# Row sums on VectorE alone with two operand blocks kept in fp32, the bias rows in GpSimd's queue, prompt rows behind a quarter of the compression weights, and the window copies one batch at a time

## What is computed

```python
shift, scale, gate = jnp.split(c @ ada_w + ada_b, 3, axis=-1)
h = rmsnorm(x, norm_g) * (1 + scale[:, None, :]) + shift[:, None, :]
return split_proj(h @ w_in), gate          # q, three K/V pairs, gates, conv inputs, z
...
k_cmp, v_cmp = compress(kc, *cmpw[:3]), compress(vc, *cmpw[3:])
lg = jnp.einsum('bqghd,bngd->bghqn', qs, k_cmp) + tab[t5_bucket(d_cmp)].transpose(2, 3, 0, 1)
...
new_kw = jnp.concatenate([buf_kw, kw], axis=1)[:, -nbuf:]
new_vw = jnp.concatenate([buf_vw, vw], axis=1)[:, -nbuf:]
```

## Time and profile before

| | us |
|---|---|
| median of three runs | 1560.9 (1558.49 to 1562.39) |
| the profiled execution | 1560.68 |
| its span, first to last instruction | 1558.9 |
| PE busy | 1440.9 (92%) |
| DVE busy | 969.7 (62%) |
| ACT busy | 704.3 (45%) |
| POOL busy | 255.4 (16%) |
| mean granted TensorE clock | 0.969 of full |

### The profile page before, as it was taken

How to read it: one execution, slowest core, us unless ns; L and a number is a source line. 1 busy time by engine, 2 the same in 40 slices (tenths; PEclk the granted TensorE clock), 3 DMA queues, 4 the chain that set the end, 5 groups by cost and what they waited for, 6 DMA issues and landing times.

```text
span 1558.9 us, 27902 instructions
## 1 busy us (share of the span) xinstructions
PE 1440.9 (92%) x10526; PEld 1242.7 (80%) x10526; DVE 969.7 (62%) x2302; ACT 704.3 (45%) x1546; POOL 255.4 (16%) x446
## 2 busy tenths in 40 slices
PE   4499988999999999949989988999998999899998
PEld 2498988999999999948777767777777776688886
DVE  2344778787887887837676646666667655553226
ACT  2222223323323233217567767777777775641111
POOL 1101332101001011031013132131131132000000
PEclk9699998999999999969999999999999999999999
DMA  9843123333333333297321231011111019973231
GB/s 353 114 131 93 31 64 86 97 76 103 83 83 110 76 89 108 51 321 233 109 90 58 59 123 40 29 45 38 28 42 42 29 38 367 253 228 94 83 98 35
DMA packets 170677, 164.76 MB, mean 106 GB/s; under 512 B 53484, under 2 KB 151916, under 8 KB 165360
## 3 DMA queue, kind: packets, MB, share of 16 engines
q1 hardware_dynamic: 155968, 97.25, 23.9%
q0 software_dynamic: 14576, 65.73, 12.4%
HBM read 131.27 MB, written 35.83 MB: 107 GB/s over the span
## 4 chain that ended last, share of the span: by engine, by line
PE 76%; DMA 7%; DVE 7%; SPq 4%; ACT 3%; issue 3%; POOL 0%; DVEq 0%; ACTq 0%; POOLq 0%
PE PS L1269 27%; PE PS L1630 11%; PE PS L1436 7%; PE PS L1401 6%; PE PS L1380 4%; PE PS L1318 4%; PE PS L1381 3%; DMA gw<-in_ada_w 2%; PE PS L1225 1%; PE PS L1226 1%; PE PS L1227 1%; DMA kb<-in_cache_k_slc,idxs 1%; PE PS L1483 1%; SPq L794 1%; DMA mixed<-mixs 1%
## 5 line engine op out<-in xcount | busy, mean ns | idle before, releaser
L1269 PE MATMUL PS<-bo,wsl 128*128 128x264 f32 x4104 | 508.2, 287 | 13.7 <-DVE qp L2180 8.3
L1269 PEld LDWEIGHTS PS<-bo,wsl 128*128 128x128 f32 x4104 | 506.4, 191 | 15.8 <-DVE qp L2180 8.7
L1890 ACT ACTIVATE pr<-PS,nm 128x640 f32<-128x640 f32 (+7 forms) x256 | 181.4, 710 | 46.3 <-DVE nm L2383 44.0
L1913 ACT ACTIVATE ptt<-PS 128x512 f32<-128x512 f32 x264 | 149.9, 602 | 47.9 <-PE PS L1401 47.6
L1726 ACT ACTIVATE wsl<-wsum 128x512 fp32r<-128x512 f32 x105 | 65.6, 630 | 228.4 <-DVE wsum L2115 228.4
L1401 PE MATMUL PS<-ident,pr 128*128 128x128 f32 x1056 | 147.6, 274 | 0.0
L1436 PE MATMUL PS<-ptt,kvt 128*64 128x256 f32 x1056 | 138.6, 394 | 3.3 <-DVE mixs L2423 3.3
L1401 PEld LDWEIGHTS PS<-ident,pr 128*128 128x128 f32 x1056 | 122.8, 141 | 8.8 <-ACT ptt L1913 0.4
L1436 PEld LDWEIGHTS PS<-ptt,kvt 128*64 128x64 f32 x1056 | 67.6, 137 | 45.2 <-issue 20.9
L2383 DVE CUSTOM_DVE_ANT_0 PS<-PS,near,nm 128x256 f32<-128x256 f32 x192 | 94.7, 493 | 6.8
L2382 DVE TENSOR_REDUCE nm<-PS 128x1 f32<-128x128 f32 (+5 forms) x128 | 70.5, 551 | 40.3 <-PE PS L1381 39.5
(11 more groups left out here) (350 smaller groups left out, 2413.0 us busy)
## 6 DMA issues: line engine op xcount, KB each, us to landing
wr<-in_w_in SPq DMA_DIRECT2D x32, 512.0 KB, 5.4
adaw<-in_ada_w SPq DMA_DIRECT2D x8, 1024.0 KB, 9.4
wr<-in_w_in SPq DMA_DIRECT2D x32, 256.0 KB, 4.4
q_stacked<-qp POOLq DMA_DIRECT2D x64, 128.0 KB, 2.7
qb<-q_stacked SPq DMA_DIRECT2D x32, 256.0 KB, 3.1
mr<-mixed SPq DMA_DIRECT2D x16, 512.0 KB, 3.9
mixed<-yy POOLq DMA_DIRECT2D x16, 264.0 KB
xb<-in_x_prompt POOLq DMA_DIRECT2D x8, 512.0 KB, 5.1
```

Of the source, the lines that this page charges most:

```text
L1269: ins = pe.matmul(PS[:, 2 * q + c, 0:H // 2], w[:, x, kk, :], b[:, y, kk, c * H // 2:(c + 1) * H // 2], start=(first and kk == 0 and x == ...
L1890: act.activation(pr[r][:, h, 0:k], score_cols(b0, w), ACT.Exp, scale=-1.0, bias=nm[:, r, h:h + 1], accum_out=rsum[:, r, h:h + 1]).then_inc ...
L1913: act.activation(pt[tc % NPT5][:, :, :], PS[:, turn_bank(c), :].rearrange("p (h c) -> p h c", h=4), ACT.Copy).then_inc(pt_act, 1)
```

## The change

Five things are altered.

1. **Bias rows.** The DMA `bias_rows<-rows` leaves SP's queue and stands in POOL's, behind the load of the last `xb` tile and ahead of the stores of kc and vc. The wait for it leaves SP's `load_w(0)` and stands before `near` on SP and before ScalarE's first write into `ca` at product (0, 5).
2. **Row sums.** POOL's `low_sums` is gone. VectorE makes `whole(O22)`, the four pieces of O22's high plus low part in fp32, in `qp` (4 instructions ahead of the gate's additions), and `whole(O11)` over them before piece 12 (4 more). A piece x < 18 is then two additions: high part with the kept piece, and the low part. Pieces 18 and 19 take three. `PIECES` is altered, and the last eight pieces are made in another order (`PIECE`), so that those which use `qp`'s upper half come first; ScalarE's `query_high` of group 2 waits for `op_sum` 16 and 18, since it writes `qp`.
3. **Prompt rows.** SP issues one quarter of the weights, then the twelve DMAs of the rows, then the other three quarters.
4. **Gather.** Quarter 1 moves from behind (23, 4) to behind (23, 6) and all of group 23's stores.
5. **Window copies.** `store_window(which, b)` copies one buffer, behind units 4 to 19; the sample's rows go behind unit 20.

```diff
         tb_mm, tb_ev, tb_rel = sem("tb_mm"), sem("tb_ev"), sem("tb_rel")
-        low_sum, op_hi = ct_pe, tb_mm
+        op_kept, op_hi = tail_t, tb_mm
...
             return tuple(m for m in prepared_at(n, i) if is_sum(m))
-        PIECES = {(0, 0): 0, (0, 1): 1, (0, 3): 2, (0, 4): 3, (0, 5): 4, (0, 7): 5, (1, 0): 6, (1, 2): 7, (1, 3): 8, (1, 4): 9,
-                  (1, 5): 10, (1, 7): 11, (2, 2): 12, (2, 3): 13, (2, 4): 14, (2, 5): 15, (2, 6): 16, (2, 7): 17, (3, 0): 18, (3, 1): 19}
+        PIECE = [(s_, k) for s_ in range(3) for k in range(HK)] + [(3, 2), (3, 3), (4, 2), (4, 3), (3, 0), (3, 1), (4, 0), (4, 1)]
+        PIECES = {(0, 0): 0, (0, 1): 1, (0, 2): 2, (0, 3): 3, (0, 4): 4, (0, 5): 5, (0, 6): 6, (0, 7): 7, (1, 0): 8, (1, 4): 9,
+                  (1, 5): 10, (1, 6): 11, (2, 2): 12, (2, 3): 13, (2, 4): 14, (2, 5): 15, (2, 6): 16, (2, 7): 17, (3, 0): 18, (3, 1): 19}
...
             sp.wait_ge(wk_ld, 32)
-            sp.wait_ge(tb_ev, 1)
-            rv = rows[:, :]
-            sp.dma_start(rowd, bass.AP(rv.tensor, rv.offset, [list(rv.ap[0]), [0, P], [1, XW]])).then_inc(row_st, 16)
...
             sp.wait_ge(wk_lo, 2)
-            sp.wait_ge(row_st, 16)
...
             sp.wait_ge(*made(NBLK - 1, 2))
-            for q in range(4):
-                load_w1(0, q)
+            load_w1(0, 0)
             sp.wait_ge(xz, 1)
...
                 load_rows(0, r)
+            for q in range(1, 4):
+                load_w1(0, q)
...
             sp.wait_ge(x3_t, 80)
+            sp.wait_ge(row_st, 16)
...
                 po.dma_start(xb[s % 2][0:rows_of(tile_at(s)), :], xp[:, s - 1, :] if s else xs).then_inc(x_ld[s % 2], 16)
+            po.wait_ge(tb_ev, 1)
+            rv = rows[:, :]
+            po.dma_start(rowd, bass.AP(rv.tensor, rv.offset, [list(rv.ap[0]), [0, P], [1, XW]])).then_inc(row_st, 16)
...
                     nout[0] += 16
-            def store_window(which):
+            def store_window(which, b):
                 dst, buf, col = ((s_kw, cache_k_win, C_KW), (s_vw, cache_v_win, C_VW))[which]
-                po.dma_start(dst[0, :, 0:WIN - TS, :, :].rearrange("b t g d -> b (t g d)"),
-                             buf[0, :, TS:WIN, :, :].rearrange("b t g d -> b (t g d)")).then_inc(out_st, 16)
-                for b in range(NB):
-                    po.dma_start(dst[0, b, WIN - TS:WIN, :, :].rearrange("t g d -> t (g d)"),
-                                 kvs[TS * b:TS * b + TS, col:col + DKV]).then_inc(out_st, 16)
-                nout[0] += 16 * 9
+                po.dma_start(dst[0, b, 0:WIN - TS, :, :], buf[0, b, TS:WIN, :, :]).then_inc(out_st, 16)
+                po.dma_start(dst[0, b, WIN - TS:WIN, :, :].rearrange("t g d -> t (g d)"),
+                             kvs[TS * b:TS * b + TS, col:col + DKV]).then_inc(out_st, 16)
+                nout[0] += 32
             store_rows(0)
...
             def gather_quarter(c, q):
-                if c == 0 and q < 2:
-                    po.wait_ge(*made(NBLK - 1, 1 if q == 0 else 4))
+                if c == 0 and q == 0:
+                    po.wait_ge(*made(NBLK - 1, 1))
...
             po.wait_ge(h_lo, NTT)
-            def low_sums(x):
-                dst, a, b, op = SUMS[x // 4]
-                if x >= 2:
-                    po.wait_ge(op_sum, x - 1)
-                po.tensor_tensor(op_scratch(x)[1][:, :], f32(bo[a][:, 1, x % 4, :]), f32(bo[b][:, 1, x % 4, :]), op).then_inc(low_sum, 1)
...
                 for i in range(products(n)):
-                    if (n, i) in PIECES:
-                        x = PIECES[n, i]
-                        if x == 0:
-                            po.wait_ge(ada_mm, 2 * KC)
-                        low_sums(x)
...
                         gather_quarter(0, 0)
-                    if n == NBLK - 1 and i == 5:
-                        gather_quarter(0, 1)
             store_za(NBLK - 1, 0)
...
             po.wait_ge(*made(NBLK - 1, 6))
+            gather_quarter(0, 1)
...
                     first(u + 1)
-                if u in (2, 5):
-                    store_window(u // 3)
-                if u == 8:
+                if 4 <= u < 4 + 2 * NB:
+                    store_window((u - 4) // NB, u % NB)
+                if u == 4 + 2 * NB:
...
                         if n == NPLAIN and i >= 2:
-                            pe.wait_ge(op_lo, {2: 4, 3: 8, 4: 16, 5: 12, 6: 20}[i])
+                            pe.wait_ge(op_lo, {2: 4, 3: 8, 4: 18, 5: 12, 6: 20}[i])
...
                 elif x >= 12:
-                    act.wait_ge(*made(2, 1))
-                act.activation(bo[SUMS[x // 4][0]][:, 0, x % 4, :], op_scratch(x)[0][:, :], ACT.Copy).then_inc(op_hi, 1)
+                    act.wait_ge(*made(2, 3 if PIECE[x][0] == 4 else 1))
+                act.activation(bo[SUMS[PIECE[x][0]][0]][:, 0, PIECE[x][1], :], op_scratch(x)[0][:, :], ACT.Copy).then_inc(op_hi, 1)
...
                     act.wait_ge(q_st, 128 * (n // 3))
+                else:
+                    act.wait_ge(op_sum, 16 if half else 18)
...
                     act.wait_ge(g_st, 16)
+                    act.wait_ge(row_st, 16)
...
                 dve.tensor_tensor(wsl[m % NSLOT][:, 1, :, :], source(m), f32(wsl[m % NSLOT][:, 0, :, :]), ALU.subtract).then_inc(w_lo, 1)
+            def whole(block):
+                for k in range(HK):
+                    ins = dve.tensor_tensor(f32(qp[:, k, :]), f32(bo[block][:, 0, k, :]), f32(bo[block][:, 1, k, :]), ALU.add)
+                ins.then_inc(op_kept, 1)
             def op_add(x):
-                dst, a, b, op = SUMS[x // 4]
+                s_, k = PIECE[x]
+                dst, a, b, op = SUMS[s_]
                 t = op_scratch(x)
...
                     dve.wait_ge(op_lo, x - 1)
-                link(dve.tensor_tensor(t[0][:, :], f32(bo[a][:, 0, x % 4, :]), f32(bo[b][:, 0, x % 4, :]), op))
-                dve.wait_ge(low_sum, 1 + x + 1)
-                dve.tensor_tensor(t[0][:, :], t[0][:, :], t[1][:, :], ALU.add).then_inc(op_sum, 1)
+                if x < 18:
+                    dve.wait_ge(op_kept, 1 if x < 12 else 2)
+                    first_, second = (f32(bo[a][:, 0, k, :]), f32(qp[:, k, :])) if s_ < 4 else (f32(qp[:, k, :]), f32(bo[b][:, 0, k, :]))
+                    link(dve.tensor_tensor(t[0][:, :], first_, second, op))
+                    dve.tensor_tensor(t[0][:, :], t[0][:, :], f32(bo[a if s_ < 4 else b][:, 1, k, :]), ALU.add).then_inc(op_sum, 1)
+                else:
+                    dve.tensor_tensor(t[0][:, :], f32(bo[a][:, 0, k, :]), f32(bo[b][:, 0, k, :]), op)
+                    link(dve.tensor_tensor(t[1][:, :], f32(bo[a][:, 1, k, :]), f32(bo[b][:, 1, k, :]), op))
+                    dve.tensor_tensor(t[0][:, :], t[0][:, :], t[1][:, :], ALU.add).then_inc(op_sum, 1)
             def op_low(x):
-                dst, t = bo[SUMS[x // 4][0]], op_scratch(x)
+                (s_, k), t = PIECE[x], op_scratch(x)
+                dst = bo[SUMS[s_][0]]
                 dve.wait_ge(op_sum, x + 1)
                 dve.wait_ge(op_hi, 1 + x + 1)
-                dve.tensor_tensor(dst[:, 1, x % 4, :], t[0][:, :], f32(dst[:, 0, x % 4, :]), ALU.subtract).then_inc(op_lo, 1)
+                dve.tensor_tensor(dst[:, 1, k, :], t[0][:, :], f32(dst[:, 0, k, :]), ALU.subtract).then_inc(op_lo, 1)
...
             link(dve.memset(uu[:, 0, 0:2], 0.0))
+            whole(O22)
...
                             op_low(x - 1)
+                        if x == 12:
+                            whole(O11)
...
                 ev_late(NBLK - 1, i)
-            dve.wait_ge(tail_t, 1)
+            dve.wait_ge(tail_t, 2 + 1)
```

## The result

The changed kernel takes 1536.06 us (median of 4 runs, 1532.23 to 1538.53) where the kernel before, on the same chip, takes 1559.7. The ratio is 0.9846, with a 95% interval of 0.9818 to 0.9874. Faster was right; the time lies above the range of 1504 to 1529. Timed once more beside other kernels it gave 1536.74 us and 0.984 (0.9813 to 0.9868).

A forecast was written before the change was run, and what follows sets the result against it. PE, busy 1440.9 of 1558.9 us, was taken as the bound, with its waits to be cut. Terms -21.8 + 3.0 - 10.7 - 12 - 6 = -47.5 on 1560.7 gave 1513 us, range 1504 to 1529.

The forecast's parts named there:

- Part 1: Projection's gates: the first gate load's 20.0 us wait and 1.8 us of slow restart go, later gate loads cost 0; -21.8 us.
- The end of the range: Gates: bound where a gate load beside the bias rows lands 10 us late, plus a slow restart; 11 us lost.
- Part 2: First products: `whole(O22)` delays the start, +3.0 us; within the stage, stretched VectorE instructions and PE gaps shrink, -10.7 us.
- Parts 3 and 4: Compression's start: prompt rows land earlier, their wait shrinks to 2 us, first `pair` at 682 to 683 us; -12 us.
- My end of -5: Compression's start, worst bound: quarter 1's gather takes the DMA engines first, weights come at 690 us; only -5 us.
- no tighter: Compression: stores needed before ScalarE's fifth step land near 687 us, after POOL's memset near 682, leaving the margin unchanged.
- Part 5: Attention: spread window copies remove PE's waits of 3.3 us on `mixs` and 2.7 us on `wide`; -6 us.
- the +12: Attention, worst bound: POOL's 1.0 us of issues shows up each time in short units; 12 us lost.
- Rivals 1 and 2: Gate loads starve beside bias rows, 1524 us, chance 0.22; compression weights come last and late, 1520, chance 0.15; both 1531.
- Rival 3: Attention: POOL's two issues in each of 16 units delay `wide`; price up to 18 us, 1531 us, chance 0.06.
- rival 4: Product (1, 0): bias rows land late for ScalarE's `ca` and the kc and vc stores; slower, 1566 us, chance 0.02.
- rival 5: Products stage: VectorE stays stretched by POOL's stores; price 11 us, 1524 us, chance 0.06.

The follow-up runs named there:

- the kernel with 16 copies: Changed kernel with 16 copies of the bias rows in place of 128, and `near` loaded as eight loads of 16 partitions; 1517.26 us, ratio 0.9721.
- `whole` was moved: Changed kernel with the four additions of `whole` for the first block put behind the four gate additions on VectorE; 1531.93 us, ratio 0.9793.
- the run with the gather held back: Changed kernel with the second quarter's gather issued only when all four quarters of the compression's first weights have landed; 1536.26 us, ratio 0.9835.
- the quarter semaphores: Changed kernel with a semaphore for each quarter of the compression's weights, so the first pair waits for the first quarter alone; 1531.04 us, ratio 0.98.
- the late copy: Changed kernel with GpSimd issuing the bias rows' copy behind the gates' store, after the last gate load; 1538.91 us, ratio 0.9844.
- the copy in two steps: Changed kernel with the bias rows copied once from SBUF to DRAM, then 127 times from DRAM to DRAM; 1525.42 us, ratio 0.9759.

## Why the prediction was wrong, point by point

**Part 1, -21.8 forecast, -6.9 measured: here the prediction failed.** The wait of 20.0 us went as said. The step that failed is "I take 0" for the three gate loads beside the bias rows. One of them, k = 5, cost 12.3 us of wait and 1.4 us of slow restart: 22.90 us from 98.38 to 121.28 and 11.96 to 133.24, where both periods are 10.58 us in the kernel with 16 copies. After the wait the clock was granted at 0.50 from 121 to 124 us. That is 13.7 us of the 14.9 that are missing; of the 14.7 us that come back with 16 copies, 1.1 us had come before the wait (its gates of k = 4 are at 97.27). The end of the range was right in its mechanism and low in its size (11 in place of 13.7). What led me wrong was the row by which I chose: small loads among gathers of 8 KB pieces late in the program said that a newcomer in SyncE's queue is served in between, where the one row of *this* copy beside a load of *this* size said 20.1 us. I set it aside because the queues were the other way round. They don't matter: 20.1 us one way, 22.25 us the other.

**Part 2.** The start: +3.0 forecast, +1.96 measured as the growth of PE's wait (2.0 less again when `whole` was moved). Within: -10.7 forecast, -8.8 measured (95.90 us from the first product to the one behind the gap, now 87.08). All stretched instructions are back at 0.7 us and one gap is left, as forecast, but of 5.76 us and not 2.4. The release named there, `qp`, is as forecast. Its size was wrong by 3.4 us, the rest of the stage made good 1.5. The cause was right too, as the row sums alone show. But the row that the prediction called in agreement does not show it: at 211.52 us VectorE began ahead of POOL's addition (211.84), so that row does not say which held the other.

**Parts 3 and 4, -12 forecast, -4.7 measured (552.7 to 548.0 us from the gap's product to the attention).** The second step that failed. The rows came on time: the wait for them is 1.5 us, 2 were forecast. The weights were issued from 660 us, and the forecast had them through some 9 us behind the tails; they took 14.06 us, and the pair stood at 16.8 us behind the tails (660.09 to 676.85). My end of -5 is where it came out; it named the gather, and the run with the gather held back shows that 6 us of the 12.4 are indeed the gather's. But a first pair on time would not have given 12 either. With the quarter semaphores it stood 7.5 us behind the tails, better than forecast, and the stage gave 8.0 us in all (552.7 to 544.7): the stores ahead of the fifth step, which the prediction called "no tighter", landed 18.2 us behind the tails (681.36, tails at 663.13), where it had them 14 behind (687 and 673.32), and PE stood 4.2 us for them. The term missed what the loads and stores do to each other while the DMA engines are 95 to 99% busy. That this load is why the weights and stores are slow is argued from the table by stretch, not shown by a run of its own.

**Part 5, -6 forecast, -8.6 measured alone.** Both waits gone, no trace of the +12. The two waits are 6.0 us of it. For the rest there is the clock, which stayed up about the second copy (1.00 for 0.94); its share was not separated. In the changed kernel the attention is 10.0 us shorter in the first profiled execution and 7.4 in the second, and there the copies would have cost more than before: with the row sums alone the wait for `mixs` is 5.6 us and not 3.3.

**Sum.** -6.9 + 1.96 - 8.8 - 4.7 = -18.4 at the attention, and the profiled executions stand 18.5 us apart there. Rivals 1 and 2 came true together; I had given the pair 1531 us and left it outside the range, and the median lies 5 us above even that. The chances were set as if the two were independent small accidents. Rival 3 (`wide` delayed), rival 4 (bias rows late for ScalarE) and rival 5 (VectorE still stretched) did not occur. In the changed kernel the copy lands at 128.2 us and ScalarE's first write of `ca` is at 164.02, so rival 4 had 36 us of cover, not 15; issued at 133.3 us, as in the late copy, it has none.

## What to carry to other kernels

Before a large copy is moved out of one load's way, list every load that runs beside its new place and price each with the row of that same copy beside a load of that size, whichever queue either stands in; then ask whether the copy can be made shorter, which was worth as much as all the reordering. Where several transfers must all land before an engine can go on, look at the DMA engines' busy share in that stretch first: if it is near one, putting one transfer ahead delays another. Then list what each later step waits for, stores included: here a wait at the fifth step took back most of what the first had gained. And when a row names a releaser, look at that instruction's own row before you explain the wait: `xt` was late for a store of 64 KB that the row of PE does not name.

## What the runs showed of the hardware

**A load in one queue waits for pieces of a copy in another before it moves at all.** In the changed kernel the gate load is issued at 99.00 us. The DMA queues from 100 to 112 us, and from 115 to 118.2 (queue, packets, MB, share of 16 engines):

```profile
q0 software_dynamic: 254, 1.17, 96.9%
```
```profile
q0 software_dynamic: 64, 0.29, 80.7%
q1 hardware_dynamic: 65, 0.27, 20.2%
```

For 14 us nothing of the load (q1) moves; then it moves one piece for one of the copy. 285 pieces went ahead up to 112.5 us, about 18 for each of 16 engines. With the copy in two steps 269 went ahead between 98.5 and 103 us, 17 for each engine, but in 4.5 us, since each takes 0.26 us and not 0.73 (share times 16 engines times length, over the pieces; the 0.18 us of one expectation is a misreading). So it is not a fixed time; whether it is a number of pieces or of bytes stays open, since both copies have pieces of 4608 B. The Trainium skill, DMA: Bandwidth & Descriptors, Queues, rings and completion order, says that each engine takes turns between its queues, a packet at a time, and that a packet is typically some 9 to 17 descriptors, 64 at most. Whether a record of the profile is such a packet or one descriptor no run here shows. If it is a packet, the second window agrees (64 and 65) and the first, with 254 and none, does not follow; if it is a descriptor, some 18 per engine ahead of the load are near one packet, and then the turns of one for one do not follow.

**Small pieces beside large ones.** In the kernel with 16 copies, from 648 to 650 us and from 656 to 658:

```profile
q1 hardware_dynamic: 1027, 0.52, 94.7%
q0 software_dynamic: 3, 0.01, 1.5%
```
```profile
q0 software_dynamic: 109, 0.80, 96.0%
q1 hardware_dynamic: 74, 0.04, 7.0%
```

The weights' 512 B pieces fall from 1027 to 74 in 2 us when the gather's large pieces come (0.80 MB in 109, 7.3 KB each). The three quarters issued from 645.16 us are 3072 such pieces; q1 had moved 2991 records by 654 us, and yet the wait for weights ended at 661.32.

**16 partitions of SBUF are a slow source.** The copy ran at 97 to 98 GB/s with the DMA engines 96% busy. From DRAM the same pieces took about a third of the time each (0.26 us for 0.73), and the copy about half (18.9 us). The Trainium skill, SBUF — State Buffer, Door 1: The DMA port swizzle, gives 104 GB/s as measured for partitions 0 to 15 against 328 for all 128. The trace agrees, with 97 GB/s; the prediction kept the copy's 35.5 us as a given and never asked why it was so long.
